# Block one of a two-model chain on one Trainium2 core: per-feature modulation sums, v first, q and k projected inside the attention steps

## The chip, the core and the metric

The kernel is one program on one core of one Trainium2 chip. Its metric is the device time in microseconds of an execution; three executions gave 2138.15 (the median), 2141.65 and 2137.65 us. All products with weights are float32 products made of three matmuls in a reduced form: each weight block and each activation is split into a high part and the rest (`hi`, `lo`), and hi·hi, hi·lo and lo·hi are accumulated in PSUM.

## The reference, cut to what matters

512 tokens of 1024 features pass a first block (adaptive modulation, differential attention with 8 heads, a mixture of 16 experts) and then a second model of two layers, whose code the change leaves alone but for semaphore numbers. Of the first block the change touches this part, and the numbering of the experts' slots:

```
mod = silu(c) @ ada_w + ada_b                # 1024 -> 6*1024
sh1, sc1, g1, sh2, sc2, g2 = split(mod, 6)
h = rmsnorm(x, norm_mix) * (1 + sc1) + sh1
q, k, v = split(h @ w_in, 3)                 # 1024 -> 3*1024
for each of 8 heads, q and k of two halves of 64:
    s1 = q1 @ k1.T / 8 + bias;  s2 = q2 @ k2.T / 8 + bias   # bias = -slope * |i - j|
    a = softmax(s1) - lam * softmax(s2)
    o = a @ v                                # head of 128 features
o = rmsnorm(o, subln) * (1 - lam_init)
x = x + g1 * (o @ w_out)
h = rmsnorm(x, norm_ffn) * (1 + sc2) + sh2
x = x + g2 * moe(h)                          # top 2 of 16 experts
```

## The kernel before, in words

Features lie on the 128 partitions, in 8 channels (`KC`) of 128, and the 512 tokens along the free axis (`x`, `h_hi`, `h_lo`: 128 x 8 x 512). Five engine programs are written out by hand and meet in counting semaphores; there is no planner. SyncE (`block.sync`) issues the loads in one fixed order: constants, parameters, router weights, `x` (2 MB), the first third of the modulation weights (`ada`, 8 MB in four loads), then the weight stream `w_a` in blocks of 128 x 1024 (512 KB) through a ring of four (`Stream.load`, L105). ScalarE makes the high part of a block (`split_hi`, L111), VectorE the low part (`split_lo`, L116), two blocks ahead of TensorE.

Stages of block one:

1. Head. ScalarE squares `x`, TensorE sums the squares (L822). VectorE multiplies the modulation weights (input features on partitions, 2048 output features along the free axis) by silu(c) and adds up over eight blocks (`ada_acc`, L1414 and L1417); TensorE adds over the partitions and turns the sum into columns with 16 one-column matmuls (L878). Only then can `normalise` make all eight channels of `h` (L1381, L1389 on VectorE, L484 on ScalarE).
2. Projections. q and k: 16 blocks, each 8 channels x 3 matmuls of 512 columns (L849 to L851), evicted by ScalarE into `qk` (L501). v: 8 blocks, with the tokens stationary (`product_t`, L867 to L869), into `v` (L510). Beside them GpSimd issues loads of the other 16 MB of modulation weights (`adb`, L1990), VectorE adds them up (`adb_acc`, L1441), and TensorE turns them at the end (L902, 32 columns).
3. Attention, 32 steps (head, block of 128 queries), in a loop of 8 steps a body. Per step: `scores` (L918, two matmuls of 64 rows and 512 columns into PSUM), `biased` on VectorE (L1471, adds the bias and takes the maximum), `exps` on ScalarE (L520), `combined` on VectorE (L1483 to L1489: both softmaxes scaled and subtracted), `turn` on TensorE (L927, four transposes), `evict_turned` on ScalarE (L527), `values` (L937), `copy_o` on VectorE (L1494), `squares_of_o` on ScalarE (L533). TensorE's order in step g is scores(g+2), turn(g+1), values(g); VectorE's is combined(g+1), biased(g+2), copy_o(g). GpSimd copies q, k and v of a head to fixed tiles and makes its bias (`stage_head`, L1999 to L2002).
4. Outputs. After the last step one Sqrt over all heads (L554), the scaling of `o` on VectorE (L1518), 32 transposes (L965), and the split into `h_hi` (L557) and `h_lo` (L1522); then the output projection (8 blocks) with the residual and the next norm.
5. Router and experts. TensorE numbers the slots of 16 experts (L1073: 4 matmuls an expert, each pair of experts behind `onehot` of VectorE, L1664). When all 16 are done, VectorE makes the row numbers (L1667 to L1674), GpSimd gathers the tokens of the first expert (L2031, L2034), TensorE turns them (L1014), and the expert products begin (L1024).

Of the kernel before, what the change touches and what calls it, by code (L numbers as in the profile page):

```python
# [19 lines left out]
F32 = mybir.dt.float32  # L20
# [12 lines left out]
H = 8  # L33
# [26 lines left out]
class Cols:  # L60
# [8 lines left out]
    def __getitem__(self, name):  # L69
# [6 lines left out]
              ("iota", P), ("slope", H), ("qkscale", 2 * H), ("pri", NG), ("tok", NT),  # L76
              ("invcount", NG * 16), ("eps", 1), ("half", 2), ("one", 1), ("pick", NT * P)])

PARAM = Cols([("c", KC), ("ada_b", 6 * KC), ("norm_mix", KC), ("norm_ffn", KC), ("norm_final", KC),
# [6 lines left out]
class Stream:  # L86
# [5 lines left out]
    def __init__(self, sem, name, src, raw, hi, lo):  # L92
        self.src, self.raw, self.hi, self.lo = src, raw, hi, lo
        self.loaded = [sem(f"{name}_loaded{s}") for s in range(SLOTS)]
# [12 lines left out]
    def split_hi(self, act, i, c):  # L107
        s = c % SLOTS
        act.wait_ge(self.loaded[s], i * 16 + 16 * (c // SLOTS + 1))
        act.wait_ge(self.used, i * SLOTS + (c + 1))  # L110
        act.activation(self.hi[:, s, :], self.raw[:, s, :], ACT.Copy).then_inc(self.hi_done, 1)  # L111
# [20 lines left out]
class ExpertStream:  # L132

    def __init__(self, sem, src, ring, hi, lo, loaded):
        self.src, self.ring, self.hi, self.lo = src, ring, hi, lo
        self.loaded = loaded + [(sem(f"m_loaded{s}"), 0) for s in range(len(loaded), RING)]
# [31 lines left out]
def build(nc, a, out):  # L168
    ctx = ExitStack()
    with ctx:  # L170
# [22 lines left out]
        cond = sb("cond", [P, KC])  # L193
# [28 lines left out]
        with ExitStack() as st:  # L222
            ada = sb("ada", [P, 4, 2, 2048], stack=st)
            ada_acc = sb("ada_acc", [P, 2048], stack=st)
        with ExitStack() as st:
            qk = sb("qk", [P, 2 * H, T], stack=st)
            v = sb("v", [P, NT, D], stack=st)
            with ExitStack() as st2:
                adb = sb("adb", [P, 2, 2 * D], stack=st2)
                adb_acc = sb("adb_acc", [P, 2, 2 * D], stack=st2)  # L230
            hd_qk = sb("hd_qk", [P, 2, 2, T], stack=st)
            hd_v = sb("hd_v", [P, 2, NT, P], stack=st)
# [74 lines left out]

        def C(name, i=0, w=None):
            s = CONST[name]
            return const[:, s] if w is None else const[:, s.start + i:s.start + i + w]  # L310
# [12 lines left out]
        sb_ = Stream(sem, "b", a["w_b"], raw, w_hi, w_lo)  # L323

        def sems(names):
            return [sem(n) for n in names.split()]

        in_const, in_x = sems("in_const in_x")
        in_ada = [sem(f"in_ada{q}") for q in range(4)]
        fetched = [sem(f"fetched{s}") for s in range(2)]  # L330
        ADB_FETCHED = 16 * KC
        sm = ExpertStream(sem, a["w_m"], ring, [w_hi[:, s] for s in range(SLOTS)] + [m_hi[:, s] for s in range(PARTS_M - SLOTS)],
                          [w_lo[:, s] for s in range(SLOTS)] + [m_lo[:, s] for s in range(PARTS_M - SLOTS)],
                          [(loaded, 16 * A_GROUPS) for loaded in sa.loaded] + [(in_x, 16), (in_const, 48)])
# [3 lines left out]
        ada_step, mod_cols, mod_done = sems("ada_step mod_cols mod_done")  # L338
        adb_step = sem("adb_step")
# [7 lines left out]
        acc_free, v_out = sems("acc_free v_out")  # L347
# [4 lines left out]
        r_ready, c_ready, a1_ready, a_ready = sems("r_ready c_ready a1_ready a_ready")  # L352
        tr_ready, pt_ready, o_ready, o_copied, o_squared = sems("tr_ready pt_ready o_ready o_copied o_squared")
        o_std_done, o_r_done, o_scaled, o_tr = sems("o_std_done o_r_done o_scaled o_tr")
# [15 lines left out]
        w2_in, q2_done, q2_sq, q2_ssq, q2_std, q2_r, q2_rrep, q2_rb, k2_done = sems(  # L370
            "w2_in q2_done q2_sq q2_ssq q2_std q2_r q2_rrep q2_rb k2_done")
        v2_done, zeroed, u2_done, wf_hi_done, wf_done = sems("v2_done zeroed u2_done wf_hi_done wf_done")
        f_mm, f_copied = sems("f_mm f_copied")
        f_step, f_exp, c_rows_done = sems("f_step f_exp c_rows_done")
# [11 lines left out]
        glu_zero, sig_done, glu_done, dve_tap, prod_done, part_step, part_done, centred, ln_silu = sems(  # L386
            "glu_zero sig_done glu_done dve_tap prod_done part_step part_done centred ln_silu")
# [5 lines left out]
        def _(sp):  # L393
            sp.dma_start(const[:], a["const"]).then_inc(in_const, 16)
            sp.dma_start(param[:], a["param"]).then_inc(in_const, 16)
            sp.dma_start(w_r[:], a["w_r"]).then_inc(in_const, 16)
            sp.dma_start(x[:], a["x"]).then_inc(in_x, 16)
            for q in range(4):
                sp.dma_start(ada[:, q], a["ada_a"][q]).then_inc(in_ada[q], 16)
            for c in range(SLOTS):  # L400
                sa.load(sp, 0, c)
            with sp.Fori(1, A_GROUPS) as i:
                for c in range(SLOTS):
                    sa.load(sp, i, c)
# [29 lines left out]
        def _(act):  # L434
# [22 lines left out]
            def sqrt_table():  # L457

                act.activation(scrap[:], C("one"), ACT.Sqrt)
# [27 lines left out]
            act.wait_ge(in_const, 48)  # L487
            act.activation(cond[:], PR("c"), ACT.Silu).then_inc(cond_done, 1)
            act.wait_ge(in_x, 16)
            rms_squares(0)  # L490
            rms_std(0)
            sa.split_hi(act, 0, 0)
            sa.split_hi(act, 0, 1)
            act.sem_inc(acc_free, 2)
            hi_parts(0, bias=lambda k: mod[:, k:k + 1])

            with act.Fori(0, 2 * H // SLOTS) as i:
                for c in range(SLOTS):
                    sa.split_hi(act, i, c + AHEAD)
                    sa.multiplied(act, i, c)  # L500
                    act.activation(qk[:, bass.ds(i * SLOTS + c, 1)], ps[:, c % 2:c % 2 + 1], ACT.Copy,  # L501
                                   scale=const[:, bass.ds(i * SLOTS + (c + CONST["qkscale"].start), 1)])\
                       .then_inc(acc_free, 1)

            for n in range(2):
                for c in range(SLOTS):
                    sa.split_hi(act, 4 + n, c + AHEAD)
                sa.multiplied(act, 4 + n, SLOTS - 1)
                for t in range(NT):
                    act.activation(v[:, t, n * T:(n + 1) * T], ps[:, 2 + t], ACT.Copy).then_inc(v_out, 1)  # L510

            act.wait_ge(lam_mm, 1)
            act.activation(lam_exp[:], ps[:, RB, 0:2], ACT.Exp).then_inc(lam_e, 1)


            def exps(i, t):

                for half in range(2):
                    act.wait_ge(nm_ready, i * 8 + (t + 1))
                    act.activation(at_p[:, t % 2 * 2 + half], at_p[:, t % 2 * 2 + half], ACT.Exp,  # L520
                                   bias=at_nm[:, t % 2, half:half + 1],
                                   accum_out=at_sum[:, t % 2, half:half + 1]).then_inc(exp_ready, 1)

            def evict_turned(i, t):
                act.wait_ge(tr_ready, i * 8 + (2 + t + 1))
                act.wait_ge(o_ready, i * 8 + (t + 1))
                act.activation(at_pt[:, t % 2], ps[:, 4 + t % 2].rearrange("p (k c) -> p k c", k=NT), ACT.Copy)\  # L527
                   .then_inc(pt_ready, 1)

            def squares_of_o(i, t):  # L530
                act.wait_ge(o_copied, i * 8 + (2 + t + 1))
                act.wait_ge(o_squared, i * 8 + (t + 1))
                act.activation(junk[:, t % 2], o[:, t % NT, bass.ds((i * 2 + t // NT) * P, P)], ACT.Square,  # L533
# [1709 lines left out]
```

## Time and profile before

| | us |
|---|---|
| median of three executions | 2138.15 |
| profiled execution, its own time | 2141.7 |
| its span | 2139.9 |
| TensorE busy (90% of the span) | 1915.9 |
| VectorE busy (57%) | 1212.9 |
| ScalarE busy (42%) | 896.4 |
| GpSimd busy (11%) | 239.6 |

How to read it: the profile is of one execution. "Busy" is the time in which an engine had an instruction in it, and for TensorE the ends are modelled. The 40 digits of the page show tenths of a slice of 53.5 us; for block one (the first eight) TensorE reads 2 8 9 8 6 6 6 9 and the granted clock 6 8 9 8 8 8 7 9 in tenths. A shape such as 128x512 is partitions by elements. x8 counts instructions, and a name in brackets with an arrow says what ended the idle time before them.

### The profile page before, as it was taken

The numbers are of one execution on the slowest core, as the hardware profiler recorded it, in microseconds if no ns is written. First come the engines' busy times: TensorE is split into PE (matmuls) and PEld (weight loads), VectorE is DVE, ScalarE is ACT, GpSimd is POOL, SyncE is SP. The second block draws the span as 40 slices with busy tenths as digits, with TensorE's granted clock in tenths as the row PEclk, the third lists the DMA queues.
The fourth block names the chain that finished last, engine by engine and source line by source line (L and its number), as shares of the span: only waits on it lengthen the run. The fifth ranks groups of instructions, "written<-read, shape, count | busy, mean of one in ns | idle before, by whom it ended". The sixth has DMA issues, their size and how long they took to land.

```text
span 2139.9 us, 27162 instructions
## 1 busy us (share of the span) xinstructions
PE 1915.9 (90%) x8674; PEld 1508.8 (71%) x8674; DVE 1212.9 (57%) x1788; ACT 896.4 (42%) x1360; POOL 239.6 (11%) x297
## 2 busy tenths in 40 slices
PE   2898666976999995998989999999999599999999
PEld 1787444775888873875656888888777377888887
DVE  4652666345888884424343666642469846666522
ACT  2222444223888873422332444431365444444311
POOL 0001120001222210003100000000057400000000
PEclk6898887966999996995569999999999789999999
DMA  7661000045999964210002222332211122223321
GB/s 303 237 245 49 1 0 1 20 155 167 354 379 381 375 261 162 99 40 10 0 0 89 76 92 96 98 118 90 78 50 60 39 76 72 95 93 97 118 94 63
DMA packets 69465, 258.52 MB, mean 121 GB/s; under 512 B 9888, under 2 KB 10016, under 8 KB 66592
## 3 DMA queue, kind: packets, MB, share of 16 engines
q1 hardware_dynamic: 61920, 230.49, 30.4%
q0 software_dynamic: 6912, 25.18, 3.2%
q10 hardware_dynamic: 576, 2.10, 0.2%
q8 instruction: 35, 0.57, 0.1%
q14 instruction: 22, 0.18, 0.0%
HBM read 253.53 MB, written 12.58 MB: 124 GB/s over the span
## 4 chain that ended last, share of the span: by engine, by line
PE 79%; DVE 9%; issue 5%; ACT 3%; DMA 2%; DVEq 0%; SPq 0%; POOL 0%; ACTq 0%; POOLq 0%
PE ps L849 17%; PE ps L851 17%; PE ps L850 17%; PE ps L1024 3%; PE ps L1026 3%; PE ps L1025 3%; PE ps L1045 1%; PE ps L1046 1%; PE ps L1044 1%; PE ps L1073 1%; DMA ada<-in_ada_a 1%; PE ps L1206 1%; PE ps L1224 1%; ACT tmp L520 1%; PE ps L867 1%
## 5 line engine op out<-in xcount | busy, mean ns | idle before, releaser
L849 PE MATMUL ps<-h_hi,w_hi 128*128 128x512 f32 x1248 | 498.3, 399 | 24.1 <-DVE w_lo L116 12.9
L850 PE MATMUL ps<-h_lo,w_hi 128*128 128x512 f32 x1248 | 491.0, 393 | 0.0
L851 PE MATMUL ps<-h_hi,w_lo 128*128 128x512 f32 x1248 | 490.8, 393 | 0.0
L116 DVE TENSOR_TENSOR w_lo<-raw,w_hi 128x1024 fp32r<-128x1024 f32 x212 | 266.2, 1260 | 269.5 <-ACT w_hi L111 264.4
L111 ACT ACTIVATE w_hi<-raw 128x1024 fp32r<-128x1024 f32 x212 | 221.3, 1050 | 217.5 <-PE ps L851 158.4
L849 PEld LDWEIGHTS ps<-h_hi,w_hi 128*128 128x128 f32 x1248 | 237.8, 191 | 80.8 <-issue 31.5
L850 PEld LDWEIGHTS ps<-h_lo,w_hi 128*128 128x128 f32 x1248 | 238.2, 191 | 50.4 <-issue 1.9
L851 PEld LDWEIGHTS ps<-h_hi,w_lo 128*128 128x128 f32 x1248 | 237.4, 190 | 50.5
L1871 DVE SCALAR_TENSOR_TENSOR tmp<-ps,param,tmp 128x511 f32<-128x511 f32 (+1 forms) x176 | 131.8, 749 | 136.0 <-ACT tmp L745 124.0
L155 DVE TENSOR_TENSOR w_lo<-ring,w_hi 128x1024 fp32r<-128x1024 f32 x128 | 149.8, 1219 | 31.9 <-ACT w_hi L151 31.8
L745 ACT ACTIVATE tmp<-ps,param 128x512 f32<-128x512 f32 x88 | 68.6, 779 | 182.0 <-PE ps L851 182.0
L849 PE MATMUL ps<-gv_hi,w_hi 128*128 (+1 forms) x352 | 138.7, 394 | 0.0
L851 PE MATMUL ps<-gv_hi,w_lo 128*128 (+1 forms) x352 | 138.0, 392 | 0.0
L850 PE MATMUL ps<-gv_lo,w_hi 128*128 (+1 forms) x352 | 136.6, 388 | 0.0
L151 ACT ACTIVATE w_hi<-ring 128x1024 fp32r<-128x1024 f32 x128 | 128.8, 1055 | 12.2 <-PE ps L1026 12.0
L1982 POOL TENSOR_TENSOR pool_carrier<-const 128x1 f32<-128x1 f32 x80 | 36.0, 449 | 810.8 <-DVE x L1895 452.2
L2117 POOL TENSOR_TENSOR part<-prod,part 128x512 f32<-128x512 f32 x64 | 87.1, 1361 | 54.5 <-ACT prod L793 50.2
L1024 PE MATMUL ps<-w_hi,e_hi 128*128 128x512 f32 x192 | 78.8, 410 | 5.1 <-DVE e_lo L1621 5.1
L155 DVE TENSOR_TENSOR m_lo<-ring,m_hi 128x1024 fp32r<-128x1024 f32 x64 | 76.5, 1217 | 2.1 <-ACT m_hi L151 2.1
L1026 PE MATMUL ps<-w_lo,e_hi 128*128 128x512 f32 x192 | 77.3, 402 | 0.0
L1025 PE MATMUL ps<-w_hi,e_lo 128*128 128x512 f32 x192 | 77.2, 402 | 0.0
L851 PEld LDWEIGHTS ps<-gv_hi,w_lo 128*128 128x128 f32 x352 | 66.1, 188 | 15.5
(308 smaller groups left out, 2877.0 us busy)
## 6 DMA issues: line engine op xcount, KB each, us to landing
ring<-in_w_m SPq DMA_DIRECT2D x192, 512.0 KB, 5.6
raw<-in_w_b SPq DMA_DIRECT2D x180, 512.0 KB, 3.3
raw<-in_w_a SPq DMA_DIRECT2D x32, 512.0 KB, 3.5
adb<-in_ada_b POOLq DMA_DIRECT2D x16, 1024.0 KB, 5.0
ada<-in_ada_a SPq DMA_DIRECT2D x4, 2048.0 KB, 20.6
y_tok<-y_dram SPq DMA_DIRECT2D x8, 512.0 KB, 7.2
x<-in_x SPq DMA_DIRECT2D x1, 2048.0 KB
h_dram<-h_tok ACTq DMA_DIRECT2D x4, 512.0 KB, 2.6
```

The lines of the kernel that those rows point to most:

```text
L111: act.activation(self.hi[:, s, :], self.raw[:, s, :], ACT.Copy).then_inc(self.hi_done, 1)
L116: dve.tensor_tensor(self.lo[:, s, :], self.raw[:, s, :], self.hi[:, s, :].bitcast(F32), ALU.subtract).then_inc(self.lo_done, 1)
L151: act.activation(self.hi[c % PARTS_M], self.ring[:, c % RING], ACT.Copy).then_inc(self.hi_done, 1)
L155: dve.tensor_tensor(self.lo[c % PARTS_M], self.ring[:, c % RING], self.hi[c % PARTS_M].bitcast(F32), ALU.subtract).then_inc(self.lo_done, 1)
L849: pe.matmul(dst, hi, a_hi, start=first, stop=False, skip_group_check=True)
L850: pe.matmul(dst, hi, a_lo, start=False, stop=False, skip_group_check=True)
L851: return pe.matmul(dst, lo, a_hi, start=False, stop=last, skip_group_check=True)
L1024: pe.matmul(ps[:, bank], e_hi[:, k], hi, start=(k == 0), stop=False, skip_group_check=True)
L1025: pe.matmul(ps[:, bank], e_lo[:, k], hi, start=False, stop=False, skip_group_check=True)
L1026: last = pe.matmul(ps[:, bank], e_hi[:, k], lo, start=False, stop=(k == KC - 1), skip_group_check=True)
L1871: dve.scalar_tensor_tensor(out=tmp[:, c, back:], in0=ps[:, c, 0:T - back], scalar=PR_at("ffn_w", it, 6, 3 * p + (f * 2 + val) * 3 * FC + tap),
L2117: pool.tensor_tensor(part[:, p], prod[:, n % 4], part[:, p], ALU.add).then_inc(part_step, 1)
```

## The change

- Modulation. The weights come transposed: 128 output features on the partitions, the 1024 input features along the free axis, and silu(c) repeated on all partitions (`cond`, 512 KB loaded). Per channel the scale is summed by one VectorE instruction (multiply and reduce), the shift by a GpSimd multiply and a ScalarE copy that accumulates. The 32 later columns are done the same way, half of them by GpSimd and ScalarE (`multiply_late`, `sum_late`), half by VectorE (`late_cols`), from the fifth channel on and inside the first 16 attention steps. SyncE issues all these loads, between those of the weight stream.
- v first, channel by channel: for each channel of `h`, 24 matmuls into eight PSUM banks, as soon as that channel is made. The rms factor is copied from PSUM to SBUF first.
- q and k are projected head by head in the order of use; half a block (12 matmuls) stands in each of the first 26 attention steps between scores and turn. All 32 steps are written out, without loops. q and k are evicted straight into the tiles of the head; v is read in place; GpSimd makes only the bias.
- `combined` no longer scales by the first softmax's sum; `copy_o` does. The transposes use one PSUM bank, q and k the last one.
- Outputs are scaled by GpSimd, turned and split in the last six steps; the last head follows inside the first two blocks of the output projection, which share the channels.
- The slots of the first two experts are numbered first, and their gathers may start then.

```
-            for q in range(4):
-                sp.dma_start(ada[:, q], a["ada_a"][q]).then_inc(in_ada[q], 16)
...
+            for f in range(KC):
+                sp.dma_start(ada[:, f], a["ada_a"][f]).then_inc(in_ada[f], 16)
+                if f < SLOTS:
+                    sa.load(sp, 0, f)
+            for c in range(SLOTS, 4 * KC):
+                sa.load(sp, c // SLOTS, c % SLOTS)
+                j = c - SLOTS
...
+                if j < 2 * KC:
+                    s = j % 2
+                    if j >= 2:
+                        sp.wait_ge(late_row, j - 1)
+                    sp.dma_start(ada_pool[:, s], a["ada_b4"][2 * j]).then_inc(in_late_pool[s], 16)
+                    if j >= 2:
+                        sp.wait_ge(late_dve, j - 1)
+                    sp.dma_start(ada_dve[:, s], a["ada_b4"][2 * j + 1]).then_inc(in_late_dve[s], 16)
... ScalarE, per channel k
+                act.wait_ge(shift_mul, k + 1)
+                act.activation(ada[:, k, 0], ada[:, k, 0], ACT.Copy, accum_out=shift_sum[:, k:k + 1]).then_inc(shift_row, 1)
...
+                act.activation(h_hi[:, k], tmp[:, k % 4], ACT.Identity, bias=mod[:, k:k + 1]).then_inc(hhi_done, 1)
+                if k >= KC // 2:
+                    sum_late(k - KC // 2)
+                sa.split_hi(act, 0, k + 1)
+            sa.split_hi(act, 0, KC + 1)
+            sum_late(KC // 2)
+            sa.split_hi(act, 0, KC + 2)
+            sum_late(KC // 2 + 1)
... and then the eight evictions of v; ScalarE, per step g
+                if g % 2 and g < 2 * KC:
+                    sum_late(KC + g // 2)
+                if g == CARRY:
+                    root_of_o(0, H - 2)
...
+                    exps(g + 2)
...
+                if g < CARRY and g % 2:
+                    evict_qk(KC + 3 + g // 2, SSQ)
+                if g <= CARRY + 2 and g % 2 == 0:
+                    sa.split_hi(act, 0, KC + 3 + g // 2 + AHEAD)
+                if g + 1 < STEPS:
+                    evict_turned(g + 1)
...
+                squares_of_o(g)
... TensorE
+            for k in range(KC):
+                sa.ready(pe, 0, k)
+                parts_made(k, 0)
...
+                for b in range(2 * NT):
+                    last = product_t(ps[:, b], sa.parts(k, b // NT, T), k, b % NT, k == 0, k == KC - 1)
...
+            for g in range(STEPS):
+                if g + 2 < STEPS:
+                    scores(g + 2)
+                if g in (28, 29, 30):
+                    turn_o(2 * (g - 28) + 1)
+                if g < CARRY:
+                    qk_part(KC + 3 + g // 2, SSQ, g % 2)
+                if g + 1 < STEPS:
+                    turn(g + 1)
+                values(g)
+                if g in (27, 28, 29):
+                    turn_o(2 * (g - 27))
... VectorE, per channel k
+                dve.tensor_tensor_reduce(out=ada[:, k, 1], in0=ada[:, k, 1], in1=cond[:], scale=1.0,
+                                         scalar=PR("ada_b", KC + k, 1), op0=ALU.mult, op1=ALU.add,
+                                         accum_out=mod[:, KC + k:KC + k + 1]).then_inc(ada_step, 1)
...
+                dve.scalar_tensor_tensor(out=tmp[:, k % 4], in0=x[:, k], scalar=scale1[:, k:k + 1], in1=rb_kept[:],
+                                         op0=ALU.mult, op1=ALU.mult).then_inc(t_done, 1)
+                sa.split_lo(dve, 0, k)
+                dve.wait_ge(hhi_done, k + 1)
+                dve.scalar_tensor_tensor(out=h_lo[:, k], in0=tmp[:, k % 4], scalar=mod[:, k:k + 1],
+                                         in1=h_hi[:, k].bitcast(F32), op0=ALU.add, op1=ALU.subtract).then_inc(hlo_done, 1)
+                if k >= KC // 2:
+                    late_cols(k - KC // 2)
... GpSimd
+            for f in range(KC):
+                pool.wait_ge(in_ada[f], 16)
+                pool.tensor_tensor(ada[:, f, 0], ada[:, f, 0], cond[:], ALU.mult).then_inc(shift_mul, 1)
+            for j in range(KC // 2):
+                multiply_late(j)
...
+            stage_bias(0)
+            stage_bias(1)
+            for j in range(KC // 2, KC):
+                multiply_late(j)
+            for h in range(2, H):
+                if h < 6:
+                    multiply_late(2 * h + 4)
+                    multiply_late(2 * h + 5)
+                stage_bias(h)
... slots on VectorE
+                slots_of(0)
+                slots_of(1)
+                dve.wait_ge(idx_ready, r * (2 * NE) + 1)
+                slot_numbers(RB, 0, 2, 0)
+                with dve.Fori(2, NE // 2) as m:
+                    slots_of(m)
+                slot_numbers(SSQ, 2, NE, 3)
```

## Rows read from the trace of the kernel before

**Rows 1.** Busy time by stretch: length, then each engine (instructions), clock, DMA share, GB/s.

```profile
0.00:59.00 59.00, 12.85 (x105) 10.36 (x105) 31.62 (x32) 16.28 (x24) 1.53 (x6) 0.67 0.68 276
59.00:191.00 132.00, 129.84 (x553) 106.79 (x554) 69.56 (x42) 35.31 (x43) 7.39 (x14) 0.97 0.61 215
...
206.00:372.00 166.00, 108.96 (x513) 69.70 (x513) 109.23 (x358) 79.06 (x227) 22.66 (x24) 0.81 0.00 0
372.00:383.00 11.00, 6.55 (x34) 6.51 (x35) 8.56 (x10) 4.56 (x7) 0.00 (x0) 0.55 0.00 0
...
466.00:495.00 29.00, 27.44 (x128) 27.38 (x128) 11.23 (x20) 5.29 (x5) 0.09 (x1) 0.50 0.54 213
495.00:511.00 16.00, 2.36 (x9) 1.97 (x10) 5.98 (x6) 2.80 (x3) 8.07 (x12) 0.50 0.48 164
```

**Rows 2.** The chain that ended last, in block one: start, us, what.

```profile
4.35 27.19 DMA ada<-in_ada_a
39.39 6.63 PE ps L878 x32
196.41 9.18 PE ps L902 x64
```

**Rows 3.** Timeline of the head: start, us, engine, line, operation, idle before.

```profile
11.97 0.20 ACT L459 ACTIVATE scrap<-const 128x1 f32<-128x1 f32 x1 [3.40 <-DMA x<-in_x]
32.84 1.06 ACT L111 ACTIVATE w_hi<-raw 128x1024 fp32r<-128x1024 f32 x1 [15.48 <-DMA raw<-in_w_a]
```

**Rows 4.** Start of the projections: timeline of two matmuls, then busy time by stretch.

```profile
64.77 0.39 PE L851 MATMUL ps<-h_hi,w_lo 128*128 128x512 f32 x1
65.00 0.40 PE L849 MATMUL ps<-h_hi,w_hi 128*128 128x512 f32 x1
...
59.00:64.00 5.00, 5.00 (x12) 3.94 (x13) 4.20 (x2) 0.00 (x0) 0.00 (x0) 0.50 0.69 210
74.00:191.00 117.00, 114.84 (x500) 94.61 (x499) 58.45 (x36) 32.57 (x40) 6.33 (x12) 0.99 0.61 216
```

**Rows 5.** Timeline of one attention step.

```profile
245.49 0.75 DVE L1489 SCALAR_TENSOR_TENSOR tmp<-tmp,at_c 128x512 f32<-128x512 f32 x1
246.16 0.69 DVE L1471 CUSTOM_DVE_ANT_0 tmp<-ps,hd_bias 128x512 f32<-128x512 f32 x1
246.29 0.66 PE L927 MATMUL ps<-const,tmp 128*128 128x128 f32 x4 [0.47 <-DVE tmp L1489]
246.79 1.06 PE L937 MATMUL ps<-hd_v,at_pt 128*128 128x128 f32 x8
247.71 0.72 ACT L520 ACTIVATE tmp<-tmp,at_nm 128x512 f32<-128x512 f32 x1
247.78 1.13 PE L918 MATMUL ps<-hd_qk 64*128 64x512 f32 x4
248.00 0.29 DVE L1494 COPY o<-ps 128x128 f32 x1 [0.33 <-PE ps L937]
```

**Rows 6.** The costliest groups: the split of weights on VectorE, busy, mean ns, idle before.

```profile
L116 DVE TENSOR_TENSOR w_lo<-raw,w_hi 128x1024 fp32r<-128x1024 f32 x212 | 266.2, 1260 | 269.5 <-ACT w_hi L111 264.4
```

**Rows 7.** VectorE beside GpSimd: timelines, then GpSimd's line 2117 with min/median/max ns.

```profile
254.60 1.85 POOL L2002 TENSOR_TENSOR hd_bias<-const 128x896 f32<-128x896 f32 x1
...
255.14 1.86 DVE L1489 SCALAR_TENSOR_TENSOR tmp<-tmp,at_c 128x512 f32<-128x512 f32 x1
...
1571.72 4.31 DVE L116 TENSOR_TENSOR w_lo<-raw,w_hi 128x1024 fp32r<-128x1024 f32 x2 [9.49 <-ACT w_hi L111]
...
L2117 POOL TENSOR_TENSOR part<-prod,part x64: 1263/1278/2368, 1564.7 to 1686.5; 128x512 f32<-128x512 f32 x64
```

**Rows 8.** Between the slots and the first expert product: timeline, and one piece of the chain.

```profile
494.60 4.63 DVE L155 TENSOR_TENSOR w_lo<-ring,w_hi 128x1024 fp32r<-128x1024 f32 x4
510.61 0.79 PE L1024 MATMUL ps<-w_hi,e_hi 128*128 128x512 f32 x1 [2.45 <-DVE e_lo L1621]
...
498.31 7.76 DMA e_x<-h_dram,src_e
```

More of the change, by code:

```diff
@@ L491, in _ @@
+            act.wait_ge(in_param, 32)
+            act.activation(cond[:], cond[:], ACT.Silu).then_inc(cond_done, 1)
+            sqrt_table()
+            act.wait_ge(in_const, 16)
             rms_std(0)
             sa.split_hi(act, 0, 0)
[L493 to L503, printed above, removed]
@@ new lines, in qk_part, with scores @@
+            def qk_part(c, bank, half):
+                if half == 0:
+                    sa.ready(pe, 0, c)
+                    if c > KC + 2:
+                        pe.wait_ge(acc_free, c - KC)
+                for k in range(KC // 2 * half, KC // 2 * (half + 1)):
+                    last = product(ps[:, bank], sa.parts(c, k), k, k == 0, k == KC - 1)
+                if half:
+                    last.then_inc(sa.used, 1)
+            def scores(g):
+                h, q = g // NT, g % NT
@@ new lines, in _ @@
+            pe.wait_ge(v_out, 1)
+            for half in range(2):
+                qk_part(KC, 0, half)
+            pe.wait_ge(v_out, NT + 3)
+            pe.wait_ge(lam_step, 2)
+            pe.matmul(ps[:, RB, LAM_AT:LAM_AT + 2], ones[0:DH, :], lam_prod[0:DH, :], start=True, stop=True,
+                      skip_group_check=True).then_inc(lam_mm, 1)
+            for half in range(2):
+                qk_part(KC + 1, 1, half)
+            pe.wait_ge(v_out, 2 * NT)
+            qk_part(KC + 2, SSQ, 0)
@@ new lines, in _ @@
+            scores(0)
+            scores(1)
+            qk_part(KC + 2, SSQ, 1)
+            turn(0)
+            for g in range(STEPS):
+                if g + 2 < STEPS:
+                    scores(g + 2)
+                if g in (28, 29, 30):
+                    turn_o(2 * (g - 28) + 1)
[6 more added lines that the diff above has]
+                    turn_o(2 * (g - 27))
@@ new lines, in last_heads @@
+            def last_heads(k):
+                if k == 3:
+                    turn_o(H - 1)
+            turn_o(H - 2)
+            pe.wait_ge(o_copied, STEPS - 1)
+            two_products(6, 0, 4, lambda k: KC, sa, last_heads)
+            for m in range(2, KC):
+                sa.ready(pe, 6, m)
+                pe.wait_ge(x_new, m - 1)
+                for k in range(KC):
+                    last = product(ps[:, 4 + m % 2], sa.parts(m, k), k, k == 0, k == KC - 1)
+                last.then_inc(sa.used, 1)
+                rms_sum(1, m - 2)
@@ L1495, in copy_o @@
                    .then_inc(o_copied, 1)
-            def attention_dve(i, more):
-                for t in range(8):
-                    if more or t + 1 < 8:
-                        combined(i, t + 1)
-                    if more or t + 2 < 8:
-                        biased(i, t + 2)
-                    copy_o(i, t)
-            biased(0, 0)
-            biased(0, 1)
-            combined(0, 0)
-            with dve.Fori(0, H // 2 - 1) as i:
-                attention_dve(i, True)
-            attention_dve(H // 2 - 1, False)
```

645 lines of the change are left out of this document (333 added, 312 removed).

## The prediction, made before the changed kernel ran

> **What bounds the kernel now.** I read first the busy time by stretch [rows 1]. TensorE is full while it projects (59 to 191 us: 129.8 of 132 us at a clock of 0.97), but in three stretches of block one it is not: the head (12.9 of 59 us), the attention (109 of 166 us at a clock of 0.81, so that part of what reads busy is work at 1.2 GHz), and the outputs (6.6 of 11 us at 0.55). Second, the chain that ended last says what each waits for [rows 2]: the head for 8 MB of modulation weights (27.2 us of DMA) and for their sum to be turned (6.6 us), and between projections and attention lie another 9.2 us of turned sums. Third, the timeline of one step [rows 5]: TensorE turns from 246.29, multiplies values from 246.79, scores from 247.78, and then waits; VectorE's combined and biased and ScalarE's exponentials fill a step of 166/32 = 5.2 us, of which TensorE needs about half. So block one has two kinds of time: TensorE at its limit, and chains in which it idles. The change lays one over the other. From the output projection on (about 383 us) only the numbering of slots is changed.
>
> **The head.** x has landed at 11.9 us, the first block of w_a at 32.8 [rows 3]; between lie 8192 + 512 KB, so 417 KB/us. In the new order x, param, cond and const (432 KB more than the old first four loads: 512 for cond, less 80 for w_r) and the first 1024 KB of ada land at 11.9 + 1456/417 = 15.4 us. Then a channel (1024 KB, with a weight block 1536) lands every 3.7 us four times and every 2.5 us after, the last at 37.5 us. DMA doesn't bound: a channel is 24 matmuls, which start 0.227 us apart (64.77 to 65.00) [rows 4], 5.45 us at 2.4 GHz.
>
> What makes a channel is VectorE: reduce (1.3 us; it is not in the trace as such; lower bound 1.2, as the 128x1024 split [rows 6], upper 2 x 0.69 [rows 5], near each other), scaling by the factor 0.75, split_lo 1.22, h_lo 0.75, and some 0.5 of small ones: 4.5 us, below TensorE's 5.45. From the fifth on late_cols adds 1.3.
>
> But GpSimd multiplies beside it, eight shifts and four late columns. Its price for 128x1024 isn't shown: lower bound 1.7 us (less than the 896 columns of 1.85), upper 2 x 1.28 = 2.55 (line 2117) [rows 7]. I take 2.1: 1.28 plus 512 columns at the slope between that row and the 896-column one, which is (1.85 - 1.28)/384, or 0.76. And the two collide. While GpSimd ran its 1.85 us multiply, VectorE's 0.75 us combination of two SBUF tiles took 1.86; two splits took 4.31 us in place of 2.45 beside GpSimd's additions [rows 7]. The biased step, with one operand in PSUM, keeps 0.69. All four large operations of a channel have both operands in SBUF now (the change copies the factor there), and so has late_cols. So I add the two engines' times instead of overlapping them: ten multiplies (21 us) fall beside the first four channels (18 us), as GpSimd runs ahead until its third late multiply waits for ScalarE's late_row; 15.4 + 39 = 54 us. Four more channels: 18, three late_cols 3.9, two multiplies 4.2: 80.5. The last channel's matmuls 5.45, less 2 us of small operations that do fit beside GpSimd: **v ends at 84 us.** The first v matmul is at about 23 us, where before it stood at 59.
>
> The Trainium skill states a rule that speaks against this placement. "SBUF — State Buffer", section "Who interferes with whom": a VectorE instruction with two SBUF inputs contends with a GpSimd instruction that reads SBUF, and the loser blocks for the whole instruction. By that rule v ends at 84, and without it at 69 (the first rival); the trace agrees in the cases named. "GPSIMD Engine Reference", section "Performance versus the Vector engine", has 4497 ns for a 2048-element fp32 tensor_tensor, so an estimate of 2.2 us for 1024; with it v would end about 1 us later.
>
> **From v to the first step.** ScalarE evicts v only behind two late sums and two splits. The second sum (j = 5) stands behind stage_bias twice (3.5 us) and two multiplies (4.2 us), which begin when the last channel's shift is known (about 76 us), with VectorE in between: about 85.5. TensorE goes on at 86.5. Three q/k blocks (16.3), the lambda matmul, two scores, a turn and small waits (4): step 0 begins at **107 us**. The 9.2 us of L902 [rows 2] go: no matmul sums columns now.
>
> **The 26 steps with a half block.** TensorE: turn 0.49 (246.29 to 246.79), values 0.99 (246.79 to 247.78), scores 1.1, 12 matmuls 2.72: 5.3 us [rows 4, 5]. VectorE: combined loses the 0.5 us scaling of 128x512 and keeps some 1.2 us, biased 1.55 (two of 0.69 and small ones), copy_o 0.3, and either a split (1.22) or, in the first 16, late_cols (1.3): 4.3. ScalarE: two exponentials 1.8 with their accumulator reads, turned 0.6, squares 0.5, and split_hi (1.06, even steps) or late sum and eviction (1.9, odd): 4 to 4.8. So TensorE is the longest, and the order allows it: after copy_o combined takes 1.2 us, while TensorE has scores and a half block (3.8) ahead of the turn, a slack of about 2 us. Where that cover is gone, every us of VectorE shows. Two waits are added. ScalarE's eviction of k comes about 0.65 us after TensorE wants the next head's scores, behind which the half block, turn and values are queued: 0.15 us a step as it falls once in four. And GpSimd has 8 multiplies and 5 biases (26 us) in the first 16 steps: a hit costs up to 2.1 us, the slack takes most; I take 0.2 a step and keep 0 and 1.3 for the range. 16 x 5.6 + 10 x 5.4 = **144 us.** The 16 MB of late weights and w_a go at 1.5 MB in two steps, far below 417 KB/us.
>
> **The last steps.** Five at 5.4 (no half block; two turns of o, two splits of 0.7 on ScalarE and VectorE each, GpSimd's scalings, and three table loads on ScalarE in place of one) and 2.5 for the last values: 29.5. The tail of 11 us [rows 1] goes: the last head is needed only at the fourth channel of the projection, 18 matmuls in (4.1 us), and its copy, squares, root and scaling take 2.3. The output projection begins at 107 + 144 + 29.5 = **280.5 us**, where before it began at 383: **-102.5 us.**
>
> **The slots.** Before, gather, turn and split come after all 16 slots: 495 to 510.6 us, 7.8 of it the DMA [rows 1, 8]. Two experts' slots take 2/16 of 28 us, so the first gather lands at about 482, under the other slots. What is late next is VectorE: small ones, four splits (4.63) and the split of tokens (1.24) behind turn and ScalarE: first product at about 501 in place of 510.6. **-10 us.** If DVE's new order stalls the slot loop, it is 0.
>
> **Sum.** 2141.7 - 102.5 - 10 = 2029 for this profiled execution; it lies 3.5 us above the median, so **2026 us.**
>
> **Rivals.**
> *A, the port doesn't matter.* GpSimd and VectorE collide at few places; channels come at TensorE's pace: v ends at 15.4 + 5.5 + 43.6 + 4 (clock rising, [rows 4]) = 69, and the steps cost 5.3 + 0.1. -15 and -5: **2006**. For it: GpSimd's multiplies are short against the stretch. Against: both rows of collisions [rows 7].
> *B, the half block isn't hidden.* ScalarE or VectorE, slowed by GpSimd and late sums, set the step, and TensorE's half block only lengthens the round: 5.0 + 2.7 = 7.7 us a step, 26 x 2.2 = 57 more: **2083**. For it: ScalarE's and VectorE's 4.3 to 4.8 are close to 5.3, and they wait for each other. Against: the slack of 2 us above.
> *C, slower: TensorE stays at 1.2 GHz.* The clock was 0.50 at the start of a full stretch and 0.81 in the attention, where TensorE paused in each step [rows 1, 4]. If the new pauses keep it at 1.2 GHz through the steps, each costs 10.6 in place of 5.3: 26 x 5.3 = 138 more: **2164**. It decides from 4.3 us a step. Against: TensorE is now busy nine tenths of a step, and at 0.99 it held [rows 4].
>
> **Chances and range.** Forecast 0.55 (its own range 2012 to 2046), A 0.26, B 0.15, C 0.04. The range of 2000 to 2062 takes in A, the bounds of the GpSimd multiply and a step of up to 6.7 us; about 0.05 lies below and 0.15 above. A measurement of this kernel tells 0.2% (4.3 us) from no change. Faster 0.95, within 0.2% 0.01, slower 0.04.
>
> **What would show it.** Right: the first product_t matmul at 20 to 25 us; VectorE splits of 2 us or more between 20 and 60 us beside GpSimd; v's last matmul at 84 against 69; steps of 5.4 to 5.6 us with a clock near 1.0; output projection at 280; first expert product about 112 us earlier than 510.6. Wrong: channels 5.5 us apart (A), steps over 6.5 us with TensorE waiting for combined (B), a clock below 0.7 in the steps (C).

## The result, and the profile after

The changed kernel takes 2065.3 us (median of four, 2057.2 to 2068.9) against 2137.9 for the kernel before (2137.5 to 2141.7) on the same chip: a ratio of 0.9651, 95% interval [0.9619, 0.9683]. That is 73 us less; 2026 were forecast with a range up to 2062, so the sign was right and the size wrong: 39 us too much was expected of it. The profiled execution took 2067.6 us, its span is 2065.8.

Busy time by stretch of the changed kernel, with the columns of [rows 1]: length, PE, PEld, DVE, ACT, POOL (instructions), granted clock, DMA share, GB/s.

```profile
0.00:26.20 26.20, 6.06 (x72) 3.35 (x73) 12.03 (x13) 14.27 (x23) 8.40 (x7) 0.75 0.93 380
26.20:91.40 65.20, 49.82 (x193) 39.51 (x193) 64.39 (x58) 28.73 (x48) 37.01 (x14) 0.89 0.68 246
91.40:112.00 20.60, 20.60 (x82) 15.38 (x82) 11.55 (x20) 10.33 (x19) 6.11 (x3) 0.92 0.41 148
112.00:154.00 42.00, 35.95 (x178) 25.17 (x176) 32.50 (x73) 24.83 (x60) 12.28 (x7) 0.96 0.38 134
154.00:196.00 42.00, 37.98 (x186) 27.10 (x185) 32.91 (x75) 22.00 (x56) 11.50 (x5) 0.96 0.42 140
196.00:277.00 81.00, 72.55 (x382) 52.39 (x381) 53.05 (x154) 45.78 (x117) 5.04 (x3) 1.00 0.17 58
277.00:313.00 36.00, 20.97 (x103) 16.47 (x102) 20.34 (x50) 19.75 (x44) 8.10 (x7) 0.72 0.09 30
```

The stages are v (26.2 to 91.4), the first q and k blocks, the steps with a half block (three lines) and the last steps (277 to 313). TensorE now runs at a clock of 0.96 to 1.00 in the steps, where the attention before had 0.81, but it is not full in the steps, and outside them it is full only in the first q and k blocks: in v VectorE is the full one (64.4 of 65.2 us), and in the last steps no engine is.

VectorE in the v stretch: start, us, line and operation. This is the third channel, from its reduction (32.06) to the next one's (46.63).

```profile
31.39 0.74 DVE L1524 SCALAR_TENSOR_TENSOR h_lo<-tmp,mod,h_hi 128x512 fp32r<-128x512 f32 x1
32.06 3.47 DVE L1509 CUSTOM_DVE_ANT_0 ada<-ada,cond,param 128x1024 f32<-128x1024 f32 x1
35.57 2.23 DVE L1513 SCALAR_TENSOR_TENSOR scale<-mod,param 128x1 f32<-128x1 f32 x1
37.83 2.83 DVE L1520 SCALAR_TENSOR_TENSOR tmp<-x,scale,rb_kept 128x512 f32<-128x512 f32 x1
40.58 3.38 DVE L117 TENSOR_TENSOR w_lo<-raw,w_hi 128x1024 fp32r<-128x1024 f32 x1
43.89 2.82 DVE L1524 SCALAR_TENSOR_TENSOR h_lo<-tmp,mod,h_hi 128x512 fp32r<-128x512 f32 x1
```

GpSimd in the same time, then min/median/max ns of its late multiplies (count, first and last start).

```profile
32.05 10.82 POOL L2115 TENSOR_TENSOR ada<-ada,cond 128x1024 f32<-128x1024 f32 x4 [2.51 <-DMA ada<-in_ada_a]
42.84 6.10 POOL L2110 TENSOR_TENSOR ada_pool<-ada_pool,cond 128x1024 f32<-128x1024 f32 x2
...
L2110 POOL TENSOR_TENSOR ada_pool<-ada_pool,cond x16: 2360/2682/3453, 42.8 to 192.5; 128x1024 f32<-128x1024 f32 x16
```

This is the collision of [rows 7], here at every instruction: each of VectorE's five takes about 2 us longer beside one multiply, even the `scale` of one column (2.23 us; 0.16 where GpSimd is idle). The channel takes 14.6 us. It is the worst of the eight: the others take 5.2 to 10.5 us, as GpSimd waits for its loads between them.

The waits between 112 and 277 us: who waited, for whom, us in total, times, longest.

```profile
ACT tmp L567 <- DVE at_nm L1556: 54.5, 26, 3.7
DVE w_lo L117 <- ACT w_hi L112: 32.9, 13, 2.5
...
PE ps L984 <- ACT hd_qk L560: 11.7, 7, 1.9
```

The second line is 13 waits of 2.5 us, one in every second step. Its place in the timeline of a step, which answers to [rows 5]:

```profile
117.99 0.71 ACT L567 ACTIVATE tmp<-tmp,at_nm 128x512 f32<-128x512 f32 x1
118.70 1.04 ACT L112 ACTIVATE w_hi<-raw 128x1024 fp32r<-128x1024 f32 x1
119.77 2.70 DVE L117 TENSOR_TENSOR w_lo<-raw,w_hi 128x1024 fp32r<-128x1024 f32 x1 [2.54 <-ACT w_hi L112]
...
122.39 0.34 DVE L1575 TENSOR_SCALAR o<-ps,at_r 128x128 f32<-128x128 f32 x1
...
123.35 0.75 DVE L1569 SCALAR_TENSOR_TENSOR tmp<-tmp,at_c 128x512 f32<-128x512 f32 x1
124.02 0.69 DVE L1550 CUSTOM_DVE_ANT_0 tmp<-ps,hd_bias 128x512 f32<-128x512 f32 x1
124.16 0.66 PE L994 MATMUL ps<-const,tmp 128*128 128x128 f32 x4 [0.26 <-DVE tmp L1569]
...
125.44 2.73 DVE L1501 CUSTOM_DVE_ANT_0 ada_dve<-ada_dve,cond,param 128x1024 f32<-128x1024 f32 x1
```

ScalarE makes the high part of the next weight block only behind its exponentials (L567), and VectorE, whose next instruction is that block's low part, stands for 2.54 us with `copy_o` (L1575), `combined` (L1569) and `biased` (L1550) queued behind it. Late `biased` makes late exponentials, then a late eviction of k, and TensorE waits for it (11.7 us, 7 times). That is most of the 18.5 us in which TensorE has no matmul in these 165 us.

The waits between 277 and 313 us, the last steps:

```profile
PE ps L1019 <- DVE h_lo L1584: 7.9, 5, 2.4
...
PE ps L994 <- DVE tmp L1569: 7.1, 1, 7.1
DVE h_lo L1584 <- ACT h_hi L593: 5.9, 2, 3.8
```

The first of the three table loads for the roots, on ScalarE, and GpSimd's scalings:

```profile
276.27 1.28 ACT L588 ACT_TABLE_LOAD   x1
...
278.64 7.05 POOL L2135 TENSOR_TENSOR o<-o,o_r 128x512 f32<-128x512 f32 x6 [26.49 <-DVE o_r L1580]
```

The turned outputs (L1019) have one PSUM bank, so each turn waits for the split of the one before it. The other two waits are one stall of 7.1 us after the root, and VectorE waiting for ScalarE's high part.

Behind the slots, answering to [rows 8] (VectorE and the first expert product):

```profile
424.98 0.22 DVE L1772 COPY slot_table<-ps 128x56 f32<-128x56 f32 x1 [2.61 <-PE ps L1164]
...
425.92 4.63 DVE L156 TENSOR_TENSOR w_lo<-ring,w_hi 128x1024 fp32r<-128x1024 f32 x4
430.46 1.22 DVE L1723 TENSOR_TENSOR e_lo<-ps,e_hi 128x1024 fp32r<-128x1024 f32 x1
...
431.82 0.79 PE L1108 MATMUL ps<-w_hi,e_hi 128*128 128x512 f32 x1 [5.07 <-DVE e_lo L1723]
```

The gather is no longer in the way; four splits are, as forecast.

### The profile page after: what moved, and what is told of

Read it like the earlier page. It is cut to its first block, busy times and chain, and to the rows that moved or that the text cites. A ratio compares the mean times of both kernels' runs of the same rounds, so it can differ in the third digit from the quotient of the medians.

```text
span 2065.8 us, 26529 instructions
## 1 busy us (share of the span) xinstructions
PE 1891.5 (92%) x8578; PEld 1482.2 (72%) x8578; DVE 1218.9 (59%) x1788; ACT 923.1 (45%) x1421; POOL 286.4 (14%) x288
## 4 chain that ended last, share of the span: by engine, by line
PE 76%; DVE 12%; issue 5%; ACT 4%; DMA 1%; SPq 0%; DVEq 0%; POOL 0%; ACTq 0%; POOLq 0%
PE ps L922 17%; PE ps L923 17%; PE ps L924 17%; PE ps L1108 3%; PE ps L1110 3%; PE ps L1109 3%; DVE w_lo L117 2%; PE ps L1424 1%; PE ps L1130 1%; PE ps L1128 1%; PE ps L1129 1%; PE ps L1297 1%; PE ps L1315 1%; PE ps L1164 1%; ACT tmp L567 1%
## 5 line engine op out<-in xcount | busy, mean ns | idle before, releaser
L117 DVE TENSOR_TENSOR w_lo<-raw,w_hi 128x1024 fp32r<-128x1024 f32 x212 | 276.0, 1306 | 253.8 <-ACT w_hi L112 248.4
L818 ACT ACTIVATE tmp<-ps,param 128x512 f32<-128x512 f32 x88 | 68.5, 778 | 183.1 <-PE ps L924 183.1
L922 PEld LDWEIGHTS ps<-gv_hi,w_hi 128*128 128x128 f32 x352 | 66.1, 188 | 16.1
L923 PEld LDWEIGHTS ps<-gv_lo,w_hi 128*128 128x128 f32 x352 | 66.1, 188 | 16.0
## 6 DMA issues: line engine op xcount, KB each, us to landing
ada<-in_ada_a SPq DMA_DIRECT2D x8, 1024.0 KB, 21.9
```

The lines of the kernel that those rows point to most:

```text
L117: dve.tensor_tensor(self.lo[:, s, :], self.raw[:, s, :], self.hi[:, s, :].bitcast(F32), ALU.subtract).then_inc(self.lo_done, 1)
L818: act.activation(tmp[:, c], ps[:, c], ACT.Identity, scale=PR_at("ffn_w", it, 6, 3 * p + (f * 2 + val) * 3 * FC + 2), bias=PR_at("ffn_b", i ...
L922: pe.matmul(dst, hi, a_hi, start=first, stop=False, skip_group_check=True)
L923: pe.matmul(dst, hi, a_lo, start=False, stop=False, skip_group_check=True)
```

## The experiments

The first four ran on one chip beside the same 13 runs of the kernel before (2138.7 us), e5 to e7 beside nine (2139.8), e8 and e9 beside nine (2141.0). Each ratio is to the kernel before.

**e1: GpSimd's multiplies take 8 of the 1024 columns** (the sums leave out the other products; all instructions and waits stay).

```
-                pool.tensor_tensor(ada[:, f, 0], ada[:, f, 0], cond[:], ALU.mult).then_inc(shift_mul, 1)
+                pool.tensor_tensor(ada[:, f, 0, 0:8], ada[:, f, 0, 0:8], cond[:, 0:8], ALU.mult).then_inc(shift_mul, 1)
... (the same in multiply_late)
```

> The changed kernel, but GpSimd's 24 multiplies by cond cover 8 of the 1024 columns, so the shift and half of the later modulation sums leave out most of their products; everything else is the same. It takes the collisions of GpSimd and VectorE away. If they set the pace of v (my forecast): channels come about 5.5 to 6 us apart, v's last matmul moves from 89 to 70 to 75 us, and the first 16 attention steps go from 6.4 to 5.8 us, so in all 24 to 30 us less than the changed kernel (about 2037). Rival: TensorE and the order of waits set the pace, GpSimd's work only fills its own idle time: v ends within 4 us of 89 and the whole within 8 us of the changed kernel.

Measured: 2032.7 us (2029.2 to 2035.2), 0.95 [0.9465, 0.9534], some 32 us below the changed kernel, a little more than the 24 to 30 expected. VectorE in v:

```profile
28.73 1.28 DVE L1509 CUSTOM_DVE_ANT_0 ada<-ada,cond,param 128x1024 f32<-128x1024 f32 x1
29.93 0.08 DVE L1509 DVE_READ_ACCUMULATOR2_ANT mod<- 128x1 f32 x1
30.05 0.16 DVE L1513 SCALAR_TENSOR_TENSOR scale<-mod,param 128x1 f32<-128x1 f32 x1
30.24 0.75 DVE L1520 SCALAR_TENSOR_TENSOR tmp<-x,scale,rb_kept 128x512 f32<-128x512 f32 x1
```

A channel takes 4.5 us (28.73 to the next at 33.22), and the last matmul of v stands at 68.5 in place of 88.6. So the multiplies cost v 20 us. The first 16 steps fall from 6.43 to 5.92 us; the waits for the high part stay (13 times in the steps, 32.9 us), so the rest of the slow steps is not the port.

**e2: the high part before the exponentials.** One pair of lines on ScalarE is moved up.

```
+                if g <= CARRY + 2 and g % 2 == 0:
+                    sa.split_hi(act, 0, KC + 3 + g // 2 + AHEAD)
                 if g + 2 < STEPS:
                     exps(g + 2)
...
-                if g <= CARRY + 2 and g % 2 == 0:
-                    sa.split_hi(act, 0, KC + 3 + g // 2 + AHEAD)
```

> The changed kernel with one thing moved: in the even attention steps ScalarE makes the high part of the next weight block before the exponentials, not behind them. In the changed kernel VectorE waits 32.9 us in 13 steps for that high part, with copy_o and combined queued behind. If that wait eats the slack and makes the eviction of k late (theory W): steps of the undisturbed part (196 to 277 us) go from 5.76 to 5.4 or 5.5, the wait for hd_qk of 11.7 us falls below 6, in all 8 to 14 us less. Rival: VectorE only waits in slack that it has anyway, and the single PSUM bank of q/k makes the wait for hd_qk: within 3 us of the changed kernel.

Measured: 2045.6 us (2039.0 to 2050.3), 0.9573 [0.9538, 0.9608]: 17 to 20 us below the changed kernel (by the ratios or by the medians), more than either theory allowed. Busy time from 113 to 255 us, with the columns of the first table:

```profile
113.00:255.00 142.00, 139.63 (x728) 101.38 (x728) 114.81 (x293) 89.45 (x226) 27.69 (x13) 1.00 0.31 112
```

TensorE is full, at full clock. The first 16 steps take 5.49 us, the next ten 5.17 (5.36, and one without a half block); VectorE's wait for the high part is gone from the list of waits, and TensorE's wait for k is 1.7 us where it was 11.7. The order of two instructions on ScalarE was what the steps lost: counted from the scores with which a step begins, the 26 steps take 141.4 us, where they took 161.1 and 144 were forecast.

**e3: outputs after the last step**, that is, no overlap: root, scaling, turns and splits follow step 31, on VectorE and ScalarE, with four PSUM banks.

```
-                if g == CARRY:
-                    root_of_o(0, H - 2)
...
+            root_of_o(0, H)
...
-                if g in (28, 29, 30):
-                    turn_o(2 * (g - 28) + 1)
...
+            for h in range(H):
+                turn_o(h)
```

> The changed kernel with its last part undone: one root over all heads after step 31, then VectorE scales, TensorE turns into four banks, both split, and the projection follows, as in the kernel before. The last five steps lose two table loads, GpSimd's scalings and the turns through one bank. My forecast had 29.5 us with the overlap against 11 us for the tail plus steps of 5.0 (27 us), 38 in all: so 8 us slower than the changed kernel. Rival: the overlap is worth nothing as it stands, since steps 26 to 30 take 8 us on average (7.1 us wait for combined at one turn, 7.9 us for h_lo at the others): within 3 us of it, or faster.

Measured: 2066.6 us (2065.2 to 2072.5), 0.9661 [0.9628, 0.9694]: the same as the changed kernel. The four intervals from the values of step 26 to those of step 30 shrink from 32.6 to 23.5 us in all, and what follows takes the difference back. The overlap of the outputs is worth nothing that these runs can tell from zero.

**e4: the kernel before with the new order of slots alone.**

```
-                with dve.Fori(0, NE // 2) as m:
...
+                slots_of(0)
+                slots_of(1)
...
+                slot_numbers(RB, 0, 2, 0)
+                with dve.Fori(2, NE // 2) as m:
+                    slots_of(m)
```

> The kernel before with only the numbering of slots changed: the first two experts' slots first, their gathers under the other slots. Forecast: first expert product about 10 us earlier, and all of it kept, as the expert stage is at TensorE's pace: -8 to -10 us against the kernel before. Rival: VectorE's new order stalls the slot loop, or the expert stage gives it back at its weights: within 3 us.

Measured: 2127.4 us (2123.1 to 2131.8, ten runs), 0.9947 [0.9931, 0.9963], 11 us faster. GpSimd's first gather, then the first expert product:

```profile
474.39 1.12 POOL L2055 DMA_INDIRECT e_x<-h_dram,src_e  x1 [0.60 <-issue]
...
501.71 0.79 PE L1024 MATMUL ps<-w_hi,e_hi 128*128 128x512 f32 x1 [5.07 <-DVE e_lo L1628]
```

The first product comes 8.9 us earlier than at 510.61 [rows 8]: this term stands by itself.

**e5: e2, and no sum through GpSimd.** VectorE reduces shift and scale of a channel itself, the 32 late columns are one VectorE reduction in each of 32 steps, and SyncE issues their loads from the 13th weight block on.

```
-                act.wait_ge(shift_mul, k + 1)
-                act.activation(ada[:, k, 0], ada[:, k, 0], ACT.Copy, accum_out=shift_sum[:, k:k + 1]).then_inc(shift_row, 1)
...
+                dve.tensor_tensor_reduce(out=ada[:, k, 0], in0=ada[:, k, 0], in1=cond[:], scale=1.0,
...
+                                         accum_out=mod[:, k:k + 1]).then_inc(shift_done, 1)
...
-                if g % 2 and g < 2 * KC:
-                    late_cols(KC + g // 2)
+                if g % 2:
+                    late_cols(g // 2)
+                else:
+                    late_a(g // 2)
```

> On e2_hi_first: no modulation sum goes through GpSimd and ScalarE any more; VectorE makes shift and scale of each channel, and all 32 later columns, one in each attention step, with their loads behind those of weight block 12. If the collision of two engines at one port cost the v stretch its 20 us: VectorE's sum a channel is 1.3 + 1.3 + 0.2 + 0.75 + 1.2 + 0.75 = 5.5 us, TensorE's pace, so v's last matmul moves from 89 to about 70, and the waits behind it shrink; steps stay at 5.4 to 5.5 although VectorE now works 5.0 us a step. In all 18 to 26 us less than e2_hi_first, about 2022. Rival: VectorE becomes the bound in the steps (6 us each): the gain in v is given back, within 8 us of e2_hi_first.

Measured: 2015.3 us (2011.3 to 2019.7), 0.9428 [0.94, 0.9457]. That is 30 us below e2 by the medians and 21 between the two profiled executions, where 18 to 26 were expected. Busy time of v, of the first q and k blocks, of the steps and of the last steps:

```profile
21.50:67.70 46.20, 45.66 (x193) 37.34 (x194) 42.10 (x59) 17.94 (x24) 3.77 (x2) 1.00 0.67 256
67.70:90.00 22.30, 21.49 (x94) 15.49 (x93) 7.96 (x22) 9.78 (x19) 0.00 (x0) 1.00 0.31 123
90.00:230.00 140.00, 139.18 (x729) 101.31 (x728) 129.91 (x328) 81.03 (x209) 10.08 (x6) 1.00 0.42 144
230.00:268.00 38.00, 21.36 (x110) 17.48 (x109) 28.71 (x63) 19.19 (x44) 9.59 (x7) 0.78 0.27 95
```

VectorE does more instructions in v than in the changed kernel and is busy for 42.1 us in place of 64.4; TensorE is full from 21.5 to 230 us. Against e2 the output projection comes 21.1 us earlier (267.6 for 288.7); 21.9 were gained when v ended. The first 16 steps take 5.37 us against 5.49: once the order is right, GpSimd's part in the sums costs 0.1 us a step.

**e6: e2 with the three roots of the outputs as Identity** (the roots are left out), so that no table is loaded for them.

```
-  act.activation(o_std[:, :, h0:h1], o_ssq[:, :, h0:h1], ACT.Sqrt, ...)
+  act.activation(o_std[:, :, h0:h1], o_ssq[:, :, h0:h1], ACT.Identity, ...)
```

> On e2_hi_first: the three roots over the outputs' squares are left out (ScalarE adds and scales without the root), so ScalarE loads no other table in steps 26 to 31. If the two extra table loads (Sqrt and back, 1.28 us each, exponentials queued behind) lengthen steps 26 and 29: 3 to 5 us less than e2_hi_first. Rival: the turns through one bank, each waiting for the h_lo before, set these steps, and the loads fall into ScalarE's waits: within 2 us.

Measured: 2038.6 us (2034.3 to 2042.8), 0.9537 [0.9508, 0.9565]. The 95% intervals of the two ratios overlap, so the times alone do not show a gain. From the first values to the output projection this execution takes 169.8 us against 172.6: about 3 us for the table loads, by one execution of each.

**e7: e2 and e3 together.** The edits are those two.

> Both edits: high part of the weights before the exponentials, and outputs scaled, turned and split only after step 31. With VectorE's wait gone the steps without the turns should take 4.9 us (VectorE's chain), and the tail 11 to 13 us: 5 x 4.9 + 13 = 37 against 36 measured in e2_hi_first from step 26 to the projection. So within 3 us of e2_hi_first, as e3 was within 2 us of the changed kernel: the overlap of the outputs is worth nothing in either. Rival: with the chain free the overlap pays its forecast 8 us, and this kernel is 5 to 8 us slower than e2_hi_first.

Measured: 2042.5 us (2038.0 to 2043.6), 0.9549 [0.9521, 0.9577], no different from e2. The last steps take 4.29, 4.28, 4.29 and 4.68 us where e2's four take 29.3 in all; the outputs then come in a row. From the first values to the output projection it is 174.4 against 172.6 us.

**e8: e5 with the outputs last.**

> The kernel of e5 (split first on ScalarE, no sum through GpSimd) with the outputs scaled, turned and split only after the last step, on VectorE and ScalarE alone, as in e7. In e5 the steps behind the last half block took 7.75, 6.92, 8.37 and 10.29 us (33.3 in all, in e2 29.3), since GpSimd's scalings ran beside VectorE's remaining late columns; in e7 they took 4.3 each. If that collision is what e5 lost in its last steps, the projection begins 4 to 8 us earlier than in e5 (267.6) and the time is 2008 to 2012 us. If the overlap of outputs is worth nothing in either order, as e7 against e2 showed within 3 us, it stays within 3 us of e5's 2015.3. If the overlap was worth something once GpSimd does nothing else, it is slower: 2018 or more.

Measured: 2016.4 us (2013.3 to 2019.9), 0.9432 [0.9409, 0.9455], no different from e5. The four last intervals take 20.1 us in place of 33.3 and the projection begins at 266.6 in place of 267.6. The collision with GpSimd's scalings was not most of what e5 lost: from the scores of step 26 to the projection it takes 39.8 us in e5 and still 38.7 here, where GpSimd scales nothing, against 35.9 in e7. The second theory stands, for the third time.

**e9: the changed kernel again**, in the session of e8.

> The changed kernel as it is, beside the same runs of the kernel before, so that the others have a measure of the same session: 2060 to 2069 us (2065.3 where it was first timed, ratio 0.965). Its first values at about 119 us and its output projection at about 314; a difference of more than 3 us in either would be the run-to-run spread of the stretch of v and q, k.

Measured: 2060.8 us (2059.6 to 2069.4), 0.9643 [0.9616, 0.967]; its first values at 118.0, the output projection at 308.6. So e8 is 44 us faster than the changed kernel beside it. The projection begins 5.1 us earlier than in the first profile, which is run-to-run spread; 3.0 of it sit in the first 16 steps (6.24 us each for 6.43). There is spread behind it too: from the first expert product to the end it is 1634.0 us in the first profile, 1632.6 here, 1629.3 before, and 1620.4 in e4, with the same instructions.

## Why the prediction was wrong, point by point

Stage by stage (us; all times are starts; a step's interval is from the first values matmul of a step to the next one's; "last four" are the intervals from step 26 to step 30, as the values of step 31 follow at once; only the forecast 84 is v's end):

| | v's last matmul | first 16 steps, each | next ten, each | last four | projection begins | first expert product |
|---|---|---|---|---|---|---|
| forecast | 84 | 5.6 | 5.4 | 21.6 | 280.5 | 398 |
| changed | 88.6 | 6.43 | 5.54 | 32.6 | 313.7 | 431.8 |
| e1 | 68.5 | 5.92 | 5.54 | 32.6 | 284.8 | 402.9 |
| e2 | 89.4 | 5.49 | 5.17 | 29.3 | 288.7 | 406.8 |
| e3 | 89.1 | 6.38 | 5.54 | 23.5 | 318.6 | 436.8 |
| e5 | 67.5 | 5.37 | 5.17 | 33.3 | 267.6 | 386.1 |
| e7 | 88.5 | 5.58 | 5.15 | 17.5 | 296.2 | 413.7 |
| e8 | 67.5 | 5.38 | 5.17 | 20.1 | 266.6 | 383.9 |

The output projection began 33.2 us later than forecast. Each step counted from its scores, as the forecast counts it, that is 7.4 until step 0 (114.4 for 107), 17.1 in the 26 steps (161.1 for 144) and 8.7 in the last part (38.2 for 29.5).

**The head and v: right in mechanism, 5 us short** (v ended at 89.0 for 84; its first matmul already stood at 26.2 for 23). Engines' times were to be added where GpSimd multiplies, and they add. A channel without GpSimd costs VectorE 4.5 us, as worked out, with the reduction at 1.28 (1.3 forecast). Too small was the multiply: 2.1 us taken, 2.36 measured at least and 2.68 at the median, which holds its own waits. The "2 us of small operations that do fit beside GpSimd" did not fit either: `scale` waits like a large one. Rival A was refuted for this kernel, and e1 made it true: 68.5 against the 69 worked out for it. The Trainium skill, "SBUF — State Buffer", section "Who interferes with whom", says that one side holds the shared ports for a whole instruction while the other blocks; these rows agree, down to the one-column instruction. The Trainium skill, "GPSIMD Engine Reference", section "Performance versus the Vector engine", leads to an estimate of 2.2 us for this multiply; the measured minimum is 2.36, and the measurement decides.

**From v to step 0.** q and k go on at 91.4, 2.4 us behind v's end, where 2.5 were forecast; but the named cause, a late sum behind the bias, was only part. The longest wait was another. SyncE's waits for VectorE's late columns between 60 and 92 us (us in total, times, longest), the chain's piece of a weight load, then ScalarE's wait for it:

```profile
SPq L428 <- DVE mod L1501: 10.7, 4, 4.4
...
83.28 5.46 DMA raw<-in_w_a
...
88.75 1.06 ACT L112 ACTIVATE w_hi<-raw 128x1024 fp32r<-128x1024 f32 x1 [6.45 <-DMA raw<-in_w_a]
```

SyncE issued this block only at 83.28, as its queue holds the late columns' loads with their waits ahead of it (the wait of 4.4 us ended just before, at 82.9), and ScalarE evicts v behind the split. The forecast priced those loads in bandwidth (0.68 of it in use) and not as waits in SyncE's queue. In e5, where these loads start later and no late column stands between VectorE's splits, q and k follow v without a gap (67.5 to 67.7). This wait was within the 2.5 us forecast. The 2.4 us that this stretch added to the miss stand behind it: from 91.4 to the scores of step 0 it is 23.0 us, where 20.5 were forecast and e5 takes 20.6; no run isolates what makes them.

**The 26 steps: this step failed.** The prediction said "TensorE is the longest, and the order allows it", with "a slack of about 2 us". The sums of busy time were right: with the order mended TensorE's steps take 5.36 us (5.3 forecast), and the slack then absorbs GpSimd. But the slack was counted from `copy_o` on as if VectorE were free to begin it. In every second step VectorE's low part stood ahead of `copy_o` and waited 2.5 us for a high part that ScalarE made behind two exponentials, which themselves begin with VectorE's maximum. So the slack was already spent. Each us of VectorE then showed, as the text had warned: GpSimd cost 0.5 us a step here (e1) and 0.1 in the mended order (e5 against e2). Mending the order gives 19.7 us in the 26 steps (161.1 to 141.4) and 17 to 20 in the whole. The wait for k, forecast at 0.65 us, was up to 1.9. This is rival B's mechanism, ScalarE and VectorE waiting for each other, at under a third of its price: 17 us and not 57.

**The last steps: failed too.** Forecast 5.4 us a step; measured 10.1, 5.3, 8.9 and 8.3. Steps with nothing beside them take 4.3 to 4.7 (e7), so four of them lost 15 us to the output work beside them, about what that work costs in a row: the projection follows the values of step 30 after 4.0 us here and after 16.0 in e7. e3, e7 and e8 show that the overlap gains nothing in any of three surroundings: with it and without, it is 38.2 and 39.9 us from the scores of step 26 to the projection (e3), 35.5 and 35.9 (e7 against e2), 39.8 and 38.7 (e8 against e5). The "tail of 11 us" went from behind the steps into them. Of the causes only the tables are isolated (about 3 us, e6). The order on ScalarE makes part of the first interval (10.1 here, 6.8 in e2). GpSimd's scalings are not the main one: six of the seven stand between 278.6 and 285.7, beside the first of the four intervals alone, and lengthen two VectorE instructions there by 0.8 to 0.9 us each. That the one PSUM bank of the turned outputs holds TensorE up is what the waits show (7.9 us here, 11.9 in e5); a second bank was not tried, as none is free while the steps run.

**The slots: right.** -9.5 us from the projection to the first product (118.1 for 127.6), -8.9 in e4; forecast -10, with VectorE's splits as what comes late next.

**The clock: right.** 0.96 to 1.00 in the steps, so rival C did not come. It fell to 0.72 in the last steps, where TensorE was busy 21 of 36 us.

**The rest.** The forecast took the program behind the slots as it was; it took 4.7 us more in this execution (1634.0 for 1629.3), within the spread seen above. 33.2 until the projection, 0.6 at the slots (118.1 for 117.5) and 4.7 here make 38.5, and 38.4 lie between the forecast 2029.2 and 2067.6.

The range reached 2062 because a step of up to 6.7 us was allowed for; that three terms would miss on the same side was not.

## What to carry to other kernels

Busy sums say whether two chains can share a step; only the order of each in-order queue says whether they do. Before counting a slack, write for each engine which instruction stands ahead of the one with the slack, and what that one waits for. Where two engines contend for ports, giving one of them less work can be worth more than dividing the work: here VectorE did all the sums alone and was done sooner, and the best version (e5 or e8, 2015 to 2016 us) is the changed kernel with the high part first and no sums through GpSimd. An overlap whose resources (one bank, one queue) belong to the steps it lies in can cost there just what it saves behind them.

## What the runs showed that was not expected

- A one-column VectorE instruction with two SBUF operands waits for a GpSimd multiply like a large one: 2.23 us for 0.16.
- The two effects were not additive in the steps: the order alone gave 0.94 us a step in the first 16 (6.43 to 5.49), the port alone 0.51, both together 1.06 (5.37, in e5, where VectorE also does GpSimd's share of the sums).
- With one span as an example of each, the 1630 us behind the first expert product vary between 1620 and 1634 with the same instructions, which is more than some of the changes that were tested; the stage-by-stage times were needed to read e6 and e7.
